# Order of masks, index scores and attention's filler work in a one-core hybrid encoder kernel

## The reference, cut to what matters

```python
h = LN0(x)                                   # 288 rows x 1024
q, k, v, q_idx, k_idx, w_idx, u = split(h @ w_in)
score[t, s] = sum_h w_idx[t, h] * relu(q_idx[t, h] . k_idx[s])   # 8 heads x 64
sel = top_k(score where s is admissible, 64 or 72 keys)
att = softmax(q . k[sel] / 8) @ v[sel]       # 8 heads share one k and v
pool = per group: (trailing mean of u - u) @ pool_w, scaled
h1 = LN1(a * h + concat(att, pool) @ w_o)
y = LN2(a * h1 + MoE(h1))                    # top 4 of 32 experts, clamped SwiGLU
```

## Time and profile before

| what | us |
|---|---|
| median of 3 runs (lowest, highest) | 1105.74 (1102.83, 1106.24) |
| the profiled execution, whole time | 1103.82 |
| its span, which the profile covers | 1101.9 |
| PE busy | 1048.7 |
| DVE busy | 393.9 |
| ACT busy | 238.7 |
| MB moved, mean rate | 421.82, 383 GB/s |

### The profile page before, as it was taken

How to read it: one execution, slowest core, us unless ns; L and a number is a source line. 1 busy time by engine, 2 the same in 40 slices (tenths; PEclk the granted TensorE clock), 3 DMA queues, 4 the chain that set the end, 5 groups by cost and what they waited for, 6 DMA issues and landing times.

```text
span 1101.9 us, 13984 instructions
## 1 busy us (share of the span) xinstructions
PE 1048.7 (95%) x5284; PEld 430.7 (39%) x5285; DVE 393.9 (36%) x697; ACT 238.7 (22%) x475; POOL 15.7 (1%) x29
## 2 busy tenths in 40 slices
PE   8989999999999999999999999999999999999996
PEld 7765453333333333333333333333333333333332
DVE  7873357322233222222233333323223223222226
ACT  3334113222221111222122222222112112212112
POOL 1003000000000000000000000000000000000000
PEclk9989899999999999999999999999999999999998
DMA  9750337999999999999999999999999999999992
GB/s 315 290 230 1 147 160 310 428 428 428 428 429 428 428 428 433 437 427 432 435 428 431 435 431 429 435 433 428 433 433 428 433 435 428 432 434 423 427 427 86
DMA packets 28556, 421.82 MB, mean 383 GB/s; under 512 B 5325, under 2 KB 5965, under 8 KB 11546
## 3 DMA queue, kind: packets, MB, share of 16 engines
q1 hardware_dynamic: 28346, 420.93, 90.4%
q10 hardware_dynamic: 192, 0.66, 0.2%
HBM read 420.11 MB, written 1.46 MB: 383 GB/s over the span
## 4 chain that ended last, share of the span: by engine, by line
PE 55%; DMA 34%; DVE 9%; issue 1%; ACT 1%; SPq 0%; DVEq 0%; ACTq 0%
DMA ring<-in_w_dram 34%; PE ps L928 29%; PE ps L954 10%; PE ps L646 4%; PE ps L773 3%; PE ps L991 2%; DVE area L1682 2%; PE ps L907 1%; DVE area L1660 1%; DVE area L1663 1%; DVE area L1656 1%; DVE area L1657 1%; PE ps L625 1%; PE ps L918 1%; DVE late L1442 1%
## 5 line engine op out<-in xcount | busy, mean ns | idle before, releaser
L928 PE MATMUL ps<-ring,area 128*64 128x512 f32 x1536 | 340.9, 594 | 15.9 <-DMA ring<-in_w_dram 15.9
L954 PE MATMUL ps<-ring,area 128*64 128x512 f32 x992 | 224.9, 595 | 0.0
L928 PEld LDWEIGHTS ps<-ring,area 128*64 128x64 f32 x1536 | 107.2, 137 | 225.9 <-issue 190.3
L1682 DVE TENSOR_TENSOR area<-area,ps 128x1024 f32<-128x1024 f32 (+1 forms) x96 | 116.5, 1214 | 55.5 <-PE ps L991 55.5
L1656 DVE TENSOR_SCALAR area<-ps 128x512 f32<-128x512 f32 x31 | 21.4, 692 | 272.2 <-PE ps L928 272.2
L928 PE MATMUL ps<-late,area 128*64 128x512 f32 x512 | 116.1, 595 | 0.0
L954 PEld LDWEIGHTS ps<-ring,area 128*64 128x64 f32 x992 | 67.5, 136 | 120.7 <-issue 118.3
L1289 ACT ACTIVATE area<-area 128x512 f32<-128x512 f32 x31 | 19.5, 629 | 404.4 <-DVE area L1656 404.4
L1648 DVE SCALAR_TENSOR_TENSOR y_sb<-ps,gcol,y_sb 64x512 fp32r<-64x512 f32 x62 | 46.5, 750 | 98.4 <-ACT y_sb L1250 98.0
L991 PE MATMUL ps<-y_sb,giveT 128*128 128x512 f32 x192 | 69.5, 444 | 11.8 <-DVE area L1682 11.8
L898 PE MATMUL ps<-area 128*64 128x512 bf16 x558 | 66.1, 382 | 0.0
(11 more groups left out here) (245 smaller groups left out, 663.5 us busy)
## 6 DMA issues: line engine op xcount, KB each, us to landing
ring<-in_w_dram SPq DMA_DIRECT2D x50, 4096.0 KB, 21.7
ring<-in_w_dram SPq DMA_DIRECT2D x60, 2048.0 KB, 16.4
late<-in_w_dram SPq DMA_DIRECT2D x10, 4096.0 KB, 26.7
late<-in_w_dram SPq DMA_DIRECT2D x12, 2048.0 KB, 15.2
area<-in_w_o_dram SPq DMA_DIRECT2D x1, 4096.0 KB, 14.1
area<-in_w_in_dram SPq DMA_DIRECT2D x1, 2560.0 KB, 16.7
area<-in_w_in_dram SPq DMA_DIRECT2D x1, 2336.0 KB, 9.4
area<-in_w_in_dram SPq DMA_DIRECT2D x1, 2048.0 KB, 20.7
```

Of the source, the lines that this page charges most:

```text
L928: last = mm(ps_gu[g * BLK:(g + 1) * BLK, c, :], x[:, spot(k), :], half_of(w, c, g), start=False, stop=(k == KT - 1))
L954: last = mm(ps_y[g * BLK:(g + 1) * BLK, :], hT[:, c, h, :], w2_t[:, h, c, g * 512:(g + 1) * 512], start=False, stop=(h == 1 and c == 3))
L1682: v.tensor_tensor(acc, acc, src[0:n, :, :], ALU.add).then_inc(done, 1)
```

## The change

Four edits, all of them in the order of work; no arithmetic is changed.

1. PE and ACT: turn_cache uses bank 0 in place of 7 and comes ahead of project(7) (it waits for relu 7 of the index); steps 8 and 9 come ahead of project(8), 10 and 11 ahead of project(9).
2. DVE: the top-k is cut in rounds. Scores 8 and 9 come behind the top-k of tile 0; then two rounds of tile 1, scores 10 and 11, two rounds, the mask of tile 0's logits, the last four rounds of tile 1 and its last step, the top-k of tile 2, inverse(0).
3. attend(t): the transpose of the reciprocals comes first (bank 3 in place of 7), behind a wait for inv_ready. In place of the three fillers stand the first three logits of the next tile, and for the last tile mix(1, pool). logits_of then computes the other five heads. ACT copies the reciprocals before the probabilities.
4. turn_x of the first pass comes ahead of last_wide, the register load of the number of passes.

```diff
@@ PE
             project(6)
             turn_kv()
+            turn_cache()
             project(7)
-            turn_cache()
-            project(8)
             index_logits(8)
             index_logits(9)
-            project(9)
+            project(8)
             index_logits(10)
             index_logits(11)
+            project(9)
...
                 pe.wait_ge(exp_done, t + 1)
                 if t >= 1:
                     pe.wait_ge(att_ready, t)
+                pe.wait_ge(inv_ready, t + 1)
+                tr(ps[0:N_HEADS, 3, 0:n], row_inv[0:n, t, :], ident[0:n, 0:n]).then_inc(invT_ps, 1)
...
-                keep_warm(3, bank=2)
+                if t < 2:
+                    logits_of(t + 1, range(3))
+                else:
+                    mix(1, pool_ks, True, False)
                 pe.wait_ge(probsT_sb, pe_groups[0])
-                pe.wait_ge(inv_ready, t + 1)
-                tr(ps[0:N_HEADS, 7, 0:n], row_inv[0:n, t, :], ident[0:n, 0:n]).then_inc(invT_ps, 1)
...
             attend(0)
-            logits_of(1)
+            logits_of(1, range(3, N_HEADS))
...
             attend(1)
-            logits_of(2)
+            logits_of(2, range(3, N_HEADS))
...
             mix(0, pool_ks, False, True)
+            pe.wait_ge(att_ready, 2)
             attend(2)
-            mix(1, pool_ks, True, False)
-            pe.wait_ge(att_ready, 2)
             mix(1, att_ks, False, True)
...
+            turn_x(x_first_sb, 1, x_gathered)
             end_wide = last_wide(pe)
-            turn_x(x_first_sb, 1, x_gathered)
@@ ACT
             exp_of(0)
             take(10)
             take(11)
+            invT_copy(0)
             probsT_copies(0)
-            invT_copy(0)
+            share_copy(0)
...
@@ DVE
-            for t in range(2):
-                hide_late_keys(t)
-                keep_top(t)
-            for i in range(8, 12):
-                index_scores(i)
+            hide_late_keys(0)
+            top_rounds(0, topk[0] // 8)
+            hide_rest(0)
+            index_scores(8)
+            index_scores(9)
+            hide_late_keys(1)
+            top_rounds(1, topk[1] // 32)
+            index_scores(10)
+            index_scores(11)
+            top_rounds(1, topk[1] // 32)
             mask_logits(0)
-            keep_top(2)
+            top_rounds(1, topk[1] // 8 - topk[1] // 32 * 2)
+            hide_rest(1)
+            top_rounds(2, topk[2] // 8)
+            hide_rest(2)
             inverse(0)
```

More of the change, by code:

```diff
@@ L668, in turn_cache @@
                 pe.wait_ge(cache_in, 48)
-                pe.wait_ge(kvrow_sb, 4)
+                pe.wait_ge(idx_relu, 7)
                 for c in range(2):
-                    last = tr(ps[:, 7, c * P:(c + 1) * P], cache_rows[:, c, :], ident[:, :])
+                    last = tr(ps[:, 0, c * P:(c + 1) * P], cache_rows[:, c, :], ident[:, :])
                 last.then_inc(cacheT_ps, 1)
@@ L698, in _, with logits_of @@
             turn_kv()
+            turn_cache()
             project(7)
-            turn_cache()
-            project(8)
             index_logits(8)
             index_logits(9)
-            project(9)
+            project(8)
             index_logits(10)
             index_logits(11)
+            project(9)
             pe.wait_ge(proj_sb, 10)
             pe.wait_ge(idx_relu, 12)
-            def logits_of(t):
+            def logits_of(t, heads=range(N_HEADS)):
                 t0, n, nk = tiles[t]
                 k0 = 0 if t < 2 else S
-                for h in range(N_HEADS):
+                for h in heads:
                     done = N_HEADS * t + h
@@ L764, in attend @@
                 last.then_inc(pv_ps, 1)
+            att_ks, pool_ks = (0, 1, 2, 3), (4, 5, 6, 7)
             def mix(t, ks, start, stop):
@@ L801, in _ @@
             last.then_inc(lastu_ps, 1)
-            att_ks, pool_ks = (0, 1, 2, 3), (4, 5, 6, 7)
             pe.wait_ge(w_o_in, 16)
@@ L1154, in cache_copies @@
                     r = slice(half * HEAD_DIM, (half + 1) * HEAD_DIM)
-                    copy(kT2[r, S:S + PAST], ps[0:HEAD_DIM, 7, 0:PAST])
-                    last = copy(kiT2[r, S:S + PAST], ps[HEAD_DIM:P, 7, 0:PAST])
+                    copy(kT2[r, S:S + PAST], ps[0:HEAD_DIM, 0, 0:PAST])
+                    last = copy(kiT2[r, S:S + PAST], ps[HEAD_DIM:P, 0, 0:PAST])
                 last.then_inc(cacheT_sb, 1)
@@ L1178, in _ @@
             kv_rows_copies()
+            cache_copies()
             take(7)
-            cache_copies()
-            take(8)
             relu_of(8)
             relu_of(9)
-            take(9)
+            take(8)
             relu_of(10)
             relu_of(11)
+            take(9)
             groups = [0]
@@ L1213, in invT_copy, with share_copy @@
                 act.wait_ge(invT_ps, t + 1)
-                copy(invT[:, 0:n], ps[0:N_HEADS, 7, 0:n]).then_inc(invT_sb, 1)
+                copy(invT[:, 0:n], ps[0:N_HEADS, 3, 0:n]).then_inc(invT_sb, 1)
+            def share_copy(t):
+                n = tiles[t][1]
                 act.wait_ge(share_done, t + 1)
@@ L1228, in _ @@
                  ps[:, 4, 0:4 * POOL_PAST].rearrange("p (g n) -> p g n", g=4)).then_inc(stateT_sb, 1)
+            invT_copy(1)
             probsT_copies(1)
-            invT_copy(1)
+            share_copy(1)
             exp_of(2)
@@ L1233, in _ @@
             copy(last_u[:, :, :], ps[0:POOL_PAST, 4:6, :]).then_inc(lastu_sb, 1)
+            invT_copy(2)
             probsT_copies(2)
-            invT_copy(2)
+            share_copy(2)
             sqrt_of(NT, (0,))
@@ L1433, in scale_rows, with top_rounds, hide_rest @@
                 v.tensor_tensor(rows[0:n, t, :], rows[0:n, t, :], lnb[0:n, 1, :], ALU.add).then_inc(ln_done, 1)
-            def keep_top(t):
+            def top_rounds(t, n_rounds):
+                _, n, nk = tiles[t]
+                sc = score[0:n, t, 0:nk]
+                for _ in range(n_rounds):
+                    link(v.max(max8[0:n, t, :], sc))
+                    link(v.match_replace(sc, max8[0:n, t, :], sc, TAKEN))
+            def hide_rest(t):
                 _, n, nk = tiles[t]
@@ L1439, in keep_top @@
                 assert topk[t] % 8 == 0
-                for _ in range(topk[t] // 8):
-                    link(v.max(max8[0:n, t, :], sc))
-                    link(v.match_replace(sc, max8[0:n, t, :], sc, TAKEN))
                 link(v.tensor_scalar(sc, sc, TAKEN / 2, HIDDEN_KEY, ALU.is_gt, ALU.mult))
```

## The result

| | before | changed |
|---|---|---|
| median, 13 runs each | 1104.22 us | 1109.14 us |
| lowest, highest | 1100.96, 1106.83 | 1106.96, 1110.97 |
| profiled execution, span | 1103.82, 1101.9 | 1109.74, 1107.7 |

The ratio is 1.0041, 95% interval 1.0032 to 1.0051: slower by 4.9 us, clear of the 0.3% that counts as no change. Run again beside other runs of before it was 1.0057 (1.0040 to 1.0075). I had forecast no change, 1105.0, with 1103 to 1107.5 for the likeliest case and 1101.0 to 1109.2 for eight in ten. 1109.14 lies outside the first and only just inside the second, at the number of the slower rival.

What follows compares the result with a forecast made beforehand. It took a fixed-length DMA stream, started at 175.67 us by PE, as the bound. +2.1 +2.2 -0.1 -0.3 -4.4 -0.3 = -0.8 us took the median from 1105.74 to 1104.9, stated as 1105.0; eight in ten 1101 to 1109.2.

Steps and rivals of the forecast that it cites:

- likeliest case: Whole kernel: the summed terms leave about no change, 1105.0 us, own range 1103 to 1107.5; chance 0.50.
- slower rival: Clock falls again inside attend(2), or once and stays down into project 12: +3.4, 1109.2 us; chance 0.20.
- reciprocal of tile 0: On DVE: waits for PE and ACT outweigh a shorter mask, so it is ready at 80.0, +2.1 us.
- clock in attend(0): PE behind 6.2 us of idling runs at the low clock: +2.2 us, bounds +1.3 and +3.0.
- mask 1, projections 12, 13: Between attend(0) and attend(1): the first mask operation of tile 1 finds its logits ready, -0.1 us.
- attend(1): Spreading follows the transposes sooner, with no wait for the inverse: -0.3 us, between 0 and -0.6.
- mask 2, first mix: Between attend(1) and attend(2): no gain or loss forecast, 0.
- tile 2: In attend(2), first mix's end to the second's takes 18.1 us instead of 22.5 at full clock: -4.4 us.
- tail: Before the first expert, transposes of x run beside the pass-count wait: -0.3 us, between 0 and -1.0.
- DVE's three gaps: DVE idles 0.8, 0.9 and 0.6 us near 52.6, 57.6 and 62.6, waiting for PE and ACT.
- the covers of the square root and the w2 loads: In tile 2, ACT's later square root (4.6 us of cover) and SP's w2 loads, issued at 141, cost nothing.
- The faster one: At tile 0 DVE keeps up or the clock rises early: +1.7 instead of +4.3, 1102.3 us; chance 0.23.

Runs made afterwards that it cites:

- e10: The changed kernel run again unaltered, with a second profile; 1109.57 us, ratio 1.0057 to before.
- e1: Changed kernel plus 27 filler matmuls on PE ahead of attend(0), where PE idles for the reciprocal; 1105.24 us, ratio 1.0006 to before.
- e6: Changed kernel with the third top-k moved behind the reciprocal, normalise and mask of tile 1; 1098.7 us, ratio 0.9955 to before.
- e7: e6 with fillers back in attend(0) and attend(1) and all eight logits behind attend; 1095.69 us, ratio 0.9922 to before.
- e3: Kernel before with only mix(1, pool) in place of the fillers of attend(2); 1100.0 us, ratio 0.9960 to before.
- e5: Kernel before with only the new order of cache transposes, index steps, top-k rounds and mask 0, attend unchanged; 1110.42 us, ratio 1.0055.
- e2: Changed kernel with the reciprocal of tile 0 moved ahead of the third top-k; 1102.2 us, ratio 0.9983 to before.

## Why the prediction was wrong, step by step

Its frame was right: the stream starts later by what PE loses ahead of 175.67, and nothing is caught up. The terms, taken at points of the chains, for the two profiles of the changed kernel (the second is e10's):

| term | forecast | first profile | second |
|---|---|---|---|
| reciprocal of tile 0 | +2.1 | +2.24 (79.98 - 77.74) | +2.3 |
| clock in attend(0) | +2.2, at most 3.0 | +4.0 (88.36 - 82.09 less 2.24) | +1.95 |
| mask 1, projections 12, 13 | -0.1 | +2.2 (102.34 - 93.90 less 6.27) | +2.65 |
| attend(1) | -0.3 | -0.3 (108.93 - 100.80 less 8.44) | -0.3 |
| mask 2, first mix | 0 | +1.1 (132.08 - 122.85 less 8.13) | 0 |
| tile 2 | -4.4 | -4.3 (18.2 less 22.5) | -4.3 |
| tail | -0.3 | -0.5 (4.4 less 4.9) | -0.5 |
| sum | -0.8 | +4.4 | +1.8 |

**The step that failed** is the price of the low clock: "I take +2.2", with "bounds +1.3 (up again after about 3 us of work) and +3.0; more than 4.1 it can't add here". I foresaw the idle PE and its length (6.2 us; 6.67 measured) and that the clock would be down behind it. I priced it in attend(0) alone and had the work behind it at -0.1 and 0. In the three rows concerned it came to 7.3 us in the first profile and 4.6 in the second, instead of 2.1. In the first the clock stayed down for 15 us after PE had work again, through attend(0), the logits and the first 2 us of project 12, and fell once more at 112. In the second attend(0) cost 1.95, within the bounds, and the clock fell again at 87.2, ahead of the logits. The earlier trace rows showed 7 us at the low level for a much shorter lull. e1 takes away the fall ahead of attend(0) and leaves the wait: 3.5 to 3.9 us.

**What the sum left out** are the falls behind the early logits. The part of the change that I had called a cover of equal worth, three logits for three fillers, takes PE's work out of the wait for normalise and mask: 1.35 us and more without an instruction ahead of L720, and a fall at five of eight such places against none of twelve without them. Between e6 and e7 this is worth 2.2 us.

**Right for the right reason** were DVE's three gaps, the reciprocal at 80.0, the idle stretch, tile 2's 18.1 (18.2, and e3 by itself 3.8 of the 4.4), the covers of the square root and the w2 loads (issued at 145.92, 141 and the 5 us by which the first mix was later than forecast), and the tail. The weight of the place was off too: I laid it to the wait's new place ahead of the transposes, and e5 idles 5.1 us and loses 5.6 by the end of the first mix without that; the place adds its part only while the clock is down.

**The rivals.** The slower one (a second fall of the clock, a low clock into project 12) named what happened and 1109.2, but put one fall in the wrong place, too late, into attend(2), where none came in any profile of a kernel with the mix there but one (e2, at 125 to 130), and I gave it 0.20. That its number was met is luck in part: it is +3.4 on a base of 1105.7, where +4.9 on 1104.2 was measured, with tile 2's gain whole. The faster one was worth 0.23 on terms of DVE that came out against it. The rule of the Trainium skill (TensorE: Matmul & The Clock Gate, What's actually happening), that the low clock is the default and activity lifts it, spoke against the change. The traces agree that the clock falls in the idle stretch (at 78.0 and, in e10, at 77.0); work lifted it only 14.8 us after it returned in the one and 3.4 us in the other. It deserved a case of its own with a chance, not a sentence.

**What stays open.** How much of the run-to-run spread is the clock's: times and mean clocks go together in every kernel with many runs (below), but no experiment held the one and varied the other. Nor is it shown why the rise came at 83.8 in one execution and at 95.1 in another of the same kernel, or why the idle stretches of 1.35 us are followed by a fall in some executions only. Parts 1 and 2 weren't tried apart, nor the wait's new place in attend by itself.

## What to carry to other kernels

If an edit makes an engine ready earlier, ask at once what it will then wait for; when that engine is PE, price the idle stretch by at least the longest low-clock stretch that the trace shows behind any lull, laid over all work behind it and not only over the piece next to it. Here that would have been half of 7 us, 3.5, still under the 4.6 and 7.3 that the two profiles show, so it is a lower bound. Work that nobody needs yet (here 9.6 us of top-k) belongs behind what somebody waits for, and it should be moved before the other pieces are packed closer. Fillers and late work that stand in PE's waits have a use that a count of instructions doesn't show: before replacing them, see which wait is left bare.

## What the runs showed of the hardware

- 6.7 us of idle PE cost 3.5 to 3.9 us through the clock alone (e1). The low level of 1.2 GHz lasted 14.8 us past the return of work in one profile, and in the other (e10) 3.4 us and, after 3.4 us at full clock, 6.8 more, while transposes, logits and products with V were what PE had.
- Idle stretches of 1.36 to 1.44 us, entered at full clock, saw a fall within them or up to 2.1 us behind in five of eight cases (e6's at 82.9 among them), those of 0.29 to 0.35 us at the same place in none of twelve.
- Mean clock and time of a run go together. Of 53 runs of the kernel before, those at 0.995 or 0.996 took 1100.4 to 1101.3 us, those at 0.990 1105.8 to 1107.0; a line through all has 1.0 us for 0.001, which is as much as the share of 1100 us itself. At 0.992 alone they range from 1102.3 to 1105.4, so the mean clock doesn't account for all of the 6 us spread, and that it causes its part isn't shown.
- The edits touch only the first 180 of 1100 us, in a kernel whose loop is a full DMA stream, and nothing of the 4.4 us was caught up: the medians differ by 4.9, and the time behind the first reload is 926.2 to 928.8 us in all twelve profiles.
